# Low parts of the second block's weights made on GpSimd instead of VectorE

## The reference

```
x = first_block(x, c, ctx, c_ctx, ...)     # two layers: modulated half FFN, attention mixer, half FFN
for l in range(2):                         # second block
    h = rms_norm(x, norm_w[l]); p = h @ w_in[l]        # split into 18 parts
    y_a = dsa_attention(...)               # index scores, top 64 keys, softmax over a latent of 128
    y_b = stick_breaking_attention(...)
    y_c = head_layer_norm(mlstm_chunkwise(silu(conv(ml_qk))...)) * sigmoid(ml_o)
    branches = [y_a * silu(dsa_z), y_b * silu(sb_z), y_c * silu(ml_z)]
    mixed = sum(sigmoid(merge) * (branches @ w_branch[l]))
    x = x + mixed @ w_out[l]
return rms_norm(x, final_norm_w)
```

## Time and profile before

| what | value |
|---|---|
| median of 3 runs | 2924.94 us (2917.83 to 2927.78) |
| the profiled execution's own time | 2923.34 us |
| its span on the core | 2921.6 us |
| mean granted TensorE clock | 0.948 |
| TensorE busy | 2612.7 us, 89% |
| VectorE busy | 1713.7 us, 59% |
| ScalarE busy | 1055.1 us, 36% |
| GpSimd busy | 0.2 us, 4 instructions |
| second block | from about 2089 us to the end |

### The profile page before, as it was taken

The page is one execution under the profiler, slowest core; times in us unless marked ns, Lnnn a source line. Parts: engine busy times, 40 slices in busy tenths (PEclk is TensorE's granted clock), DMA queues, the critical chain, the costliest instruction groups (busy, mean ns, idle before and its releaser), DMA issues.

```text
span 2921.6 us, 36731 instructions
## 1 busy us (share of the span) xinstructions
PE 2612.7 (89%) x14702; PEld 2197.9 (75%) x14702; DVE 1713.7 (59%) x3456; ACT 1055.1 (36%) x1742; POOL 0.2 (0%) x4
## 2 busy tenths in 40 slices
PE   2799999798789999979999968899898987998968
PEld 2588777487458887848888856799897957998748
DVE  8777743426848776358623355555556547556466
ACT  1222222424742222242222255544543443444433
POOL 0000000000000000000000000000000000000000
PEclk9999999899999999999999989899999988999889
DMA  6344432021014444214422210255343402444302
GB/s 242 121 183 182 162 130 101 29 92 54 1 61 173 173 173 159 101 44 174 176 97 101 89 71 29 92 188 187 137 174 130 173 1 101 166 159 147 113 1 87
DMA packets 48553, 348.77 MB, mean 119 GB/s; under 512 B 5376, under 2 KB 5504, under 8 KB 6528
## 3 DMA queue, kind: packets, MB, share of 16 engines
q1 hardware_dynamic: 48384, 346.43, 32.4%
HBM read 345.36 MB, written 1.05 MB: 119 GB/s over the span
## 4 chain that ended last, share of the span: by engine, by line
PE 78%; DVE 16%; ACT 3%; issue 2%; DMA 1%; SPq 0%; DVEq 0%; ACTq 0%
PE ps L376 22%; PE ps L378 21%; PE ps L377 21%; DVE hr L1312 4%; PE ps L428 3%; PE ps L418 1%; PE ps L490 1%; PE ps L492 1%; PE ps L491 1%; DVE yT L1284 1%; PE ps L533 1%; DMA ring<-in_wk 1%; DVE uT L1264 1%; DVE w_lo L1238 1%; DVE u_lo L1253 1%
## 5 line engine op out<-in xcount | busy, mean ns | idle before, releaser
L1238 DVE TENSOR_TENSOR w_lo<-ring,w_hi 128x1024 fp32r<-128x1024 f32 x504 | 617.0, 1224 | 765.5 <-ACT w_hi L868 763.8
L868 ACT ACTIVATE w_hi<-ring 128x1024 fp32r<-128x1024 f32 x504 | 534.0, 1060 | 1412.6 <-PE ps L378 1357.1
L376 PE MATMUL ps<-u_hi,w_hi 128*128 128x512 f32 (+1 forms) x1744 | 648.4, 372 | 51.8 <-DVE u_lo L1253 51.7
L378 PE MATMUL ps<-u_hi,w_lo 128*128 128x512 f32 (+1 forms) x1744 | 637.8, 366 | 0.0
L377 PE MATMUL ps<-u_lo,w_hi 128*128 128x512 f32 (+1 forms) x1744 | 635.2, 364 | 0.0
L376 PEld LDWEIGHTS ps<-u_hi,w_hi 128*128 128x128 f32 x1744 | 333.4, 191 | 115.8 <-DVE u_lo L1253 47.3
L1312 DVE SCALAR_TENSOR_TENSOR hr<-ring,cond,hr 128x256 f32<-128x256 f32 x1008 | 405.0, 477 | 0.0
L378 PEld LDWEIGHTS ps<-u_hi,w_lo 128*128 128x128 f32 x1744 | 333.5, 191 | 54.6
L377 PEld LDWEIGHTS ps<-u_lo,w_hi 128*128 128x128 f32 x1744 | 333.8, 191 | 51.1 <-issue 0.2
L376 PE MATMUL ps<-uh,w_hi 128*128 128x256 f32 x1184 | 339.4, 287 | 27.1 <-ACT zt L1140 17.0
L377 PE MATMUL ps<-ul,w_hi 128*128 128x256 f32 x1184 | 334.5, 282 | 0.0
(11 more groups left out here) (267 smaller groups left out, 2943.3 us busy)
## 6 DMA issues: line engine op xcount, KB each, us to landing
ring<-in_wk SPq DMA_DIRECT2D x324, 1024.0 KB, 4.8
hT<-in_x SPq DMA_DIRECT2D x1, 2048.0 KB, 10.1
htabs<-in_htabs SPq DMA_DIRECT2D x1, 1152.0 KB, 7.2
out_t<-uT SPq DMA_DIRECT2D x1, 1024.0 KB, 3.9
trig<-in_trig SPq DMA_DIRECT2D x3, 256.0 KB, 5.0
wuk<-in_uk SPq DMA_DIRECT2D x2, 256.0 KB, 5.0
wuv<-in_uv SPq DMA_DIRECT2D x2, 256.0 KB, 5.2
cols<-in_cols SPq DMA_DIRECT2D x1, 302.5 KB, 2.9
```

The costliest lines, as they stand in the source:

```text
L376: mm(bank, hi, x_hi, start=first, stop=False)
L378: return mm(bank, lo, x_hi, start=False, stop=last)
L868: f(half_hi(K, 0, HALF), ringed(n, K % 2 * HALF, (K % 2 + 1) * HALF), ACT.Copy).then_inc(whi_ready, 1)
L1238: tt(half_lo(K, 0, HALF), ringed(HALF_SLOT[K], K % 2 * HALF, (K % 2 + 1) * HALF), half_hi(K, 0, HALF).bitcast(F32), ALU.subtract).then_inc ...
```

## The change

The first 316 halves keep their lows on VectorE. For the last 188, VectorE's calls of `low()` do nothing, and a new program on GpSimd makes each low as soon as its high is there. Nothing else is changed.

```
+BLOCK2 = HALVES - 94 * DEPTH
...
             def low():

                 nonlocal K
-                if K < HALVES:
+                if K < BLOCK2:
                     dve.wait_ge(whi_ready, K + 1)
                     tt(half_lo(K, 0, HALF), ringed(HALF_SLOT[K], K % 2 * HALF, (K % 2 + 1) * HALF),
                        half_hi(K, 0, HALF).bitcast(F32), ALU.subtract).then_inc(wlo_ready, 1)
...
-            assert H == K == HALVES
+            assert H == HALVES and K == BLOCK2
+
+        @block.gpsimd
+        def _(pool):
+
+            pool.wait_ge(wlo_ready, BLOCK2)
+            for k in range(BLOCK2, HALVES):
+                pool.wait_ge(whi_ready, k + 1)
+                nc.gpsimd.tensor_tensor(half_lo(k, 0, HALF), ringed(HALF_SLOT[k], k % 2 * HALF, (k % 2 + 1) * HALF),
+                                        half_hi(k, 0, HALF).bitcast(F32), ALU.subtract).then_inc(wlo_ready, 1)
```

## The result

The changed kernel takes 2939.55 us (median of 8 runs, 2932.63 to 2945.14) against 2923.32 (8 runs, 2917.83 to 2928.88): 1.0053 times as long, interval 1.0037 to 1.0069, or +16 us. The direction and the range of the prediction held; the forecast was +21. The profiled execution went from 2921.6 to 2933.6 us, +12.0. Its second block begins 6.2 us earlier (TensorE's first column there, the 24 matmuls of one half, at 2082.92 instead of 2089.10, by code that is the same), so the second block took 18.2 us more.

The account below looks back on a forecast made before the run. TensorE was taken as the bound (78% of the chain), with VectorE ending its waits in places; 2 x (3.7 + 1.8 + 5.0) = +21.0 us gave 2946 us, range 2903 to 2962.

Parts of the forecast that it names:

- The size of a low: One GpSimd low of 1024 columns: 2.3 us taken, between VectorE's 1.22 and the 2.82 us pace of a half.
- the pace rival: GpSimd's low takes over 2.82 us and about 148 halves pay the excess: 2973 us at 3.0; chance 0.10.
- The exclusion: A GpSimd low and VectorE operations at doubled rate or with two SBUF operands exclude each other, whole instruction against whole instruction.
- Tap sums: Convolution: sums start earlier, but five lows put 12.0 us into the chain, ending at 2250.8 us; +3.7 us a layer.
- that stays: TensorE's restart after the tap sums keeps its granted clock of 0.63, two halves taking 8.5 instead of 5.65 us.
- Last rope: Last rotation before the index scores: its second product and sum wait for GpSimd lows, ending at 2195.5 us; +1.8 a layer.
- Values: Value projection, counted among the full TensorE stretches, where GpSimd lows were to cost nothing.
- at 2.3 the full stretches ... cost nothing: With lows of 2.3 us, stretches where TensorE is full, about 74 halves a layer, lose no time.
- high and low have two halves, 5.65 us: Full projection: a high starts three halves ahead, so its low may last 4.4 us before TensorE waits once.
- Branches: Branch stretch: last group 2.8 us longer over four halves, middle group 2.0, last mixed lows 0.2; +5.0 a layer.
- The faster one: Rival of no or partial exclusion: conv ends at 2238.8, TensorE's restart is not slow; 2896 us in full; chance 0.25.
- Its partial form: Only doubled-rate operations collide, 8 of 32 tap operations; conv gains 4.7 us and the total is 2906 us.

Follow-up runs that it names:

- the PSUM experiment: Changed kernel with all 32 tap operations a layer reading their addend from a PSUM tile, convolution values left out: 2920.75 us, 0.9999 of the kernel before.
- quarters: Changed kernel with each GpSimd low made as four instructions of 256 columns: 2920.46 us, 0.9996 of the kernel before.
- copies: Kernel before, lows on VectorE, with four idle GpSimd copies of 240 columns after each high in layer 0, memsets in layer 1: 2930.56 us, 1.0025.

## Why the prediction was right, and where it was off

**The size of a low.** 2.3 taken, 2.41 measured (2.34 to 2.65). The Trainium skill (GPSIMD Engine Reference, Performance versus the Vector engine) gave 1.96 times VectorE's, 2.4, which is the nearer; the pace rival is out, with highs still 2.82 us apart. By the prediction's own slope (+21 at 2.3 us, +32 at 2.8) the longer low is worth 2 us more.

**The exclusion.** Inferred from a half stream missing in rows 7, and shown by the groups above and by the PSUM experiment. The Trainium skill (SBUF — State Buffer, Who interferes with whom) says whole instruction, and for lows of one instruction this case agrees: 10.9 us of 12.0. For quarters and copies the runs show less than the instruction's length (0.39 of 0.76, 0.18 of 0.63), and there the measurement decides.

**Tap sums, +3.7 a layer; measured +1.5 and +1.6.** The end came 2.6 us later relative to the stage's start, not 3.7: the five lows held the sums for 10.9 us and not 12.0. The step that failed in size is "that stays": the restart's clock did not stay. In layer 0 two halves took 7.30 us at 0.73 instead of 8.50 at 0.63, which takes 1.2 off again. Why a longer stand was followed by a higher clock no run shows.

**Last rope, +1.8; measured +1.45** in TensorE's stand. What the step left out is the restart behind it: 5.80 us at 0.54 instead of 5.00 at 0.66 in layer 0, and in layer 1, where the stand of 2.5 us had been followed by full speed, a first column of 5.16 instead of 3.44. This is all of the index stage's +0.9 and +1.7; as told above, in layer 1 some half of it is the luck of the profile before.

**Values, 0 predicted, +2.1 a layer.** This is the step "at 2.3 the full stretches ... cost nothing", and under it "high and low have two halves, 5.65 us". It reckoned with one half used up after the other at an even pace. The values use two halves over two token tiles. The high of a slot's second half can start only when the first half of the slot before is done, 1.4 us ahead of the slot (2164.66 for a slot that starts at 2166.06), and TensorE needs its low at the fifth chunk of the first tile, 1.41 us into the slot. So high and low have 2.8 us and not 5.65. The slot behind the projections has no such slot before it, and is on time: three of four are late. Before, that low ended 0.55 us ahead of this point. Now it ends 2168.18 - 2166.06 = 2.12 us into the slot, 0.71 late; 0.43 of this shows as TensorE's idle time in the timeline, and the slot's first token tile takes 0.7 us longer (3.90 instead of 3.18 from tile to tile), three times a layer. What decides is not the mean pace, but the least slack of any half.

**Branches, +5.0; measured +5.5 and +5.3.** First group -0.2 and -0.4 (0 predicted), second 1.75 (2.0), third 3.26 (2.8), the output's restart 0.74 (0.2).

**The sum.** Predicted 21.0 = 2 x 10.5. In the stages it is +23.9. That the two are so near is in part luck: the tap sums came 4.4 us short over both layers, and the values, which the prediction had at nothing, brought 4.2. The projection and attention stretches gave 5.7 back in the profile (their length differs by as much between profiles of kernels with the same code there), so +18.2 in the block and +16 in the medians. The exclusion and its places are shown; of the 8 us between stages and medians some 0.8 are the short index column before, and the rest is not accounted for by any cause.

**The rivals.** The faster one failed at its condition, not at its price: five lows hold the tap sums for 10.9 us, more than its 8.2. Its partial form, a collision of the doubled-rate operations alone, is out by L1583, which is not one of them and went from 485 to 844 ns. The prediction also called the index scores' operations single-input or covered: the score sums have two SBUF operands and are held (2598 ns), and covered they are.

## What to carry to other kernels

Before work is moved from VectorE to GpSimd, list the VectorE operations beside which it would run: those with two SBUF operands or at doubled rate stood still here for about as long as a GpSimd low lasts, with everything behind them in the queue. If the move is wanted, short GpSimd instructions hold less than one long one (here all of the loss, for a fifth more GpSimd time), and an operation with one operand in PSUM is not held. Check also where a low has the least slack, and not only the mean pace. Better is to ask first whether the late work must stand where it is: moving the tap sums into a stretch where TensorE is full gave 0.72%, with no engine changed.

## What the runs showed of the hardware that was not expected

- A GpSimd subtraction of 256 columns repeats every 0.69 us where VectorE is not in its way (five in 3.47 us) and one of 1024 takes 2.41, yet it holds VectorE for 0.39 against 2.2 us: a quarter of the length is less than a quarter of the hold.
- GpSimd itself hardly gives way: over 188 lows none took more than 2.65 us (median 2.41), beside VectorE operations that stood for up to 2.2 us. Its quarters do give way: 0.76 us on average and up to 1.12, against 0.69.
- TensorE's 24 matmuls of a projection column repeat every 2.827 us in some stretches and every 2.720 in others, in the same kernel (after the tap sums of layer 0 at 2.827 before and at 2.720 after), which makes 2.5 us in such a stretch. What picks the one or the other stays open.
- The attention stretch, which uses no weights of the stream, took between 106.7 and 115.2 us over these profiles. Where it was looked up, the longer ones had the lower granted clock: 0.57 over the first 44 us in the two of 115.2, against 0.77 before. That is as large as the effect studied, and why stages are compared here rather than spans.
